# Head norms, rotary items and latent projections placed inside the mixers' input projection

## The reference

```python
    for l in range(DEPTH_2):
        x = x + 0.5 * swiglu(rms_norm(x, ffn1_norm[l]), ffn1_w_gate[l], ffn1_w_up[l], ffn1_w_down[l])
        h = rms_norm(x, mix_norm[l])
        pa, pb, pc, pd = jnp.split(h @ w_in[l], IN_SPLITS, axis=-1)
        ya = neighbourhood_mixer(pa, na_q_norm[l], na_k_norm[l], na_rpb[l], na_beta[l])
        yb = mla_mixer(pb, mla_q_lat_norm[l], mla_w_uq[l], mla_kv_lat_norm[l], mla_w_ukv[l],
                       mla_q_norm[l], mla_k_norm[l], mla_beta[l], ang_seq)
        yc = diff_mixer(pc, diff_q_norm[l], diff_k_norm[l], diff_lambda[l], diff_subln[l],
                        t5_bias, diff_lambda_init(l))
        yd = gqa_mixer(pd, gqa_q_norm[l], gqa_k_norm[l], gqa_beta[l], ang_row, ang_col)
        x = x + jnp.concatenate([ya, yb, yc, yd], axis=-1) @ w_out[l]
...
def mla_mixer(p, q_lat_norm, w_uq, kv_lat_norm, w_ukv, q_norm, k_norm, beta, ang):
    c_q, c_kv, k_rope = jnp.split(p, [MLA_Q_RANK, MLA_Q_RANK + MLA_KV_RANK], axis=-1)
    q = (rms_norm(c_q, q_lat_norm) @ w_uq).reshape(b, s, MLA_HEADS, MLA_NOPE + MLA_ROPE)
    kv = (rms_norm(c_kv, kv_lat_norm) @ w_ukv).reshape(b, s, MLA_HEADS, MLA_NOPE + MLA_V)
...
    q = rms_norm(q, q_norm)
    k = rms_norm(k, k_norm)
    q = jnp.concatenate([q[..., :MLA_NOPE], apply_rope(q[..., MLA_NOPE:], ang)], axis=-1)
    k = jnp.concatenate([k[..., :MLA_NOPE], apply_rope(k[..., MLA_NOPE:], ang)], axis=-1)
```

## Time and profile before

| what | value |
|---|---|
| median of 3 runs | 3502.92 us |
| lowest and highest run | 3497.03 and 3503.17 us |
| the profiled execution, its own time | 3499.19 us |
| span of the profiled execution | 3497.4 us |
| mean granted clock of TensorE | 0.957 of full |
| busy share: TensorE, VectorE, ScalarE, GpSimd | 95%, 50%, 37%, 6% |

### The profile page before, as it was taken

The page is one execution under the profiler, slowest core; times in us unless marked ns, Lnnn a source line. Parts: engine busy times, 40 slices in busy tenths (PEclk is TensorE's granted clock), DMA queues, the critical chain, the costliest instruction groups (busy, mean ns, idle before and its releaser), DMA issues.

```text
span 3497.4 us, 41394 instructions
## 1 busy us (share of the span) xinstructions
PE 3337.3 (95%) x15399; PEld 2655.9 (76%) x15399; DVE 1740.9 (50%) x2604; ACT 1299.6 (37%) x1853; POOL 213.4 (6%) x234
## 2 busy tenths in 40 slices
PE   8989987999999999999889999999999988999998
PEld 6667865888888888876478888878887646978887
DVE  7354467445553455333565555445553256555532
ACT  4226645224332333322247333333322233733322
POOL 1001100000000000010120100010001002010000
PEclk9959998999999999999789999999999987999999
DMA  5310012333333333332102333333333311223332
GB/s 125 96 42 4 1 55 67 97 91 96 96 94 94 101 96 94 89 106 67 47 20 65 95 97 95 89 94 96 96 95 93 91 53 17 67 73 97 98 94 67
DMA packets 518249, 275.12 MB, mean 79 GB/s; under 512 B 39523, under 2 KB 510407, under 8 KB 517986
## 3 DMA queue, kind: packets, MB, share of 16 engines
q1 hardware_dynamic: 513154, 262.77, 27.0%
q0 software_dynamic: 3600, 9.85, 0.9%
q10 hardware_dynamic: 1360, 0.66, 0.1%
HBM read 262.70 MB, written 2.14 MB: 76 GB/s over the span
## 4 chain that ended last, share of the span: by engine, by line
PE 89%; DVE 7%; ACT 2%; issue 1%; DMA 0%; POOL 0%; DVEq 0%; ACTq 0%; POOLq 0%
PE bank L375 24%; PE bank L377 24%; PE bank L376 24%; PE bank L1004 5%; PE bank L985 4%; PE bank L993 3%; PE bank L896 1%; PE bank L690 1%; PE bank L804 1%; DVE wlo L351 1%; PE bank L1679 1%; DVE xc L1886 0%; ACT whi L344 0%; DVE q L932 0%; DVE hhi L2183 0%
## 5 line engine op out<-in xcount | busy, mean ns | idle before, releaser
L375 PE MATMUL bank<-hhi,whi 128*128 128x512 f32 (+1 forms) x2528 | 1004.3, 397 | 38.0 <-DVEq L415 20.9
L376 PE MATMUL bank<-hhi,wlo 128*128 128x512 f32 (+1 forms) x2528 | 990.7, 392 | 0.0
L377 PE MATMUL bank<-hlo,whi 128*128 128x512 f32 (+1 forms) x2528 | 990.3, 392 | 0.0
L351 DVE TENSOR_TENSOR wlo<-raw,whi 128x1024 fp32r<-128x1024 f32 x485 | 607.2, 1254 | 621.9 <-ACT whi L344 613.3
L344 ACT CAST whi<-raw 128x1024 fp32r<-128x1024 f32 x485 | 505.0, 1046 | 428.4 <-PE bank L377 413.1
L375 PEld LDWEIGHTS bank<-hhi,whi 128*128 128x128 f32 (+1 forms) x2528 | 476.9, 189 | 184.2 <-issue 79.1
L376 PEld LDWEIGHTS bank<-hhi,wlo 128*128 128x128 f32 (+1 forms) x2528 | 477.3, 189 | 102.6 <-issue 3.5
L377 PEld LDWEIGHTS bank<-hlo,whi 128*128 128x128 f32 (+1 forms) x2528 | 476.8, 189 | 102.8
L375 PE MATMUL bank<-uhi,whi 128*128 128x512 f32 x880 | 348.9, 396 | 0.0
L376 PE MATMUL bank<-uhi,wlo 128*128 128x512 f32 x880 | 348.3, 396 | 0.0
L377 PE MATMUL bank<-ulo,whi 128*128 128x512 f32 x880 | 348.3, 396 | 0.0
(11 more groups left out here) (432 smaller groups left out, 3589.3 us busy)
## 6 DMA issues: line engine op xcount, KB each, us to landing
raw<-in_ffn_w_gate SPq DMA_DIRECT2D x88, 512.0 KB, 3.9
raw<-in_ffn_w_up SPq DMA_DIRECT2D x88, 512.0 KB, 3.7
raw<-in_w_in SPq DMA_DIRECT2D x78, 512.0 KB, 3.8
raw<-in_ffn_w_down SPq DMA_DIRECT2D x64, 512.0 KB, 3.9
raw<-in_w_out SPq DMA_DIRECT2D x24, 512.0 KB, 4.1
raw<-in_ffn_w_down SPq DMA_DIRECT2D x32, 384.0 KB, 3.4
raw<-in_w_gate SPq DMA_DIRECT2D x22, 512.0 KB, 3.9
raw<-in_w_up SPq DMA_DIRECT2D x22, 512.0 KB, 3.7
```

The source lines that it names most:

```text
L351: k.nc.vector.tensor_tensor(k.wlo[:, slot, :], k.raw[:, slot, :], k.whi[:, slot, :].bitcast(F32), ALU.subtract)\
L375: mm(out, whi, hi(kc), start=start and i == 0, stop=False)
L376: mm(out, wlo, hi(kc), start=False, stop=False)
L377: last = mm(out, whi, lo(kc), start=False, stop=stop and i == kcs - 1)
```

## The change

Parts 1 to 3 of `mix` become one stage without a handover inside, `mixer_inputs`. It has 22 units: three of B's latents, A's four queries and keys, B's rotary key (unit 7, `KR`), the two short latent units (8 and 9, `UQ`, `UKV`), D's, C's, and last the values (17 to 21). Each unit has two places for side work, called slots: slot 2u after half of unit u's matmuls, slot 2u+1 after the unit. Tables say what stands in which slot: `sums` (square sums), `spreads`, `rotations` (one slot behind the spread of a rotary item), `turns` (slots 20 to 23 for B's values, 36 to 39 for A's, 40, 42 and 44 for C's and D's), and the scales in four groups of heads (`roots`, `inverses`, `parts`). Every engine walks through the 45 slots in the same order. Spreads have one bank instead of two, transposes one instead of two. The latents' parts have buffers of their own, since `hhi` and `hlo` are in use. VectorE no longer copies the values' channels of the latents, ScalarE does. The cosine goes straight into the item's tile. The copies that gathered A's values on ScalarE are now four reads of the bank on VectorE for each of two units. The t5 table is loaded when the last unit is done, and GpSimd's bias additions wait for it. The exponential of lambda is in slot 41.

```diff
-        for c in range(4):
-            block(m2, 0, KC, O_A + c * P, P)
         for c in range(3):
             block(m2, 0, KC, O_B + c * P, P)
         for c in range(4):
-            block(m2, 0, KC, O_C + c * P, P)
+            block(m2, 0, KC, O_A + c * P, P)
+        block(m2, 0, KC, O_B + 384 - 64, 96)
+        block(rows_by_chunk(w["mla_w_uq_2"][l]), 0, 2, 0, 4 * MD)
+        block(rows_by_chunk(w["mla_w_ukv_2"][l]), 0, 1, 0, 4 * P)
...
+                    mixer_inputs(k, w, l, (qA, kA, vA), (qB, kB, vB), (qC, kC, vC), (qD, kD, vD), lat_parts, lam, gain,
+                                 lambda name, shape, dt=F32: sb(name, shape, dt, mem))
...
-            latent_heads(k, w, l, kr, qB, kB, vB, gain)
-            handover(k)
...
     def _(pool):
+        pool.wait_ge(*k.t5_landed.all())
         pool.wait_ge(*loaded)
...
+def mixer_inputs(k, w, l, near, latent, diff, shared, lat_parts, lam, gain, sb):
...
+    KR, UQ, UKV, VALUES, UNITS = 7, 8, 9, 17, 22
...
+    norm_of = {0: 11, 1: 12, 2: 13, 3: 0, 4: 1, 5: 2, 6: 3, 10: 8, 11: 9, 12: 10, 13: 4, 14: 5, 15: 6, 16: 7}
+    normed = [0, 1, 2, 3, 4, 5, 6] + [None] * 8 + [10, 11, 12, 13, 14, 15, 16]
+    sums = {2 * u + 3: [normed.index(u)] for u in norm_of}
+    sums.update({17 + i: [7 + 2 * i, 8 + 2 * i] for i in range(4)})
+    firsts, lasts = (0, 3, 7, 15), (2, 6, 14, 21)
+    group = lambda i: sum(i >= f for f in firsts) - 1
+    roots, inverses, parts = {7: 0, 15: 1, 21: 2, 35: 3}, {7: 0, 19: 1, 21: 2, 35: 3}, {8: 0, 20: 1, 22: 2, 36: 3}
...
+    spreads = {9 + i: i for i in range(3)}
+    spreads.update({21 + i: 3 + i for i in range(12)})
+    spreads.update({37 + i: 15 + i for i in range(7)})
+    rotations = {s + 1: i - 7 for s, i in spreads.items() if items[i]["rope"]}
...
+        def slot(s):
+            if s in rotations:
+                r = rotations[s]
+                rows = rope(r)["rows"]
+                pe.wait_ge(*k.xn_done.at(7 + r + 1))
+                if r >= 1:
+                    pe.wait_ge(*k.rope_sin.at(r))
+                if r == 8:
+                    pe.wait_ge(*gqa_ready)
+                nc.tensor.matmul(rotated[0:rows, :], rot[0:rows, 0:rows], tmp[0:rows, r % 2, :], start=True, stop=True)\
+                    .then_inc(*k.rot_done.up())
+            if s in spreads:
+                i = spreads[s]
+                it, g = items[i], group(i)
+                if i == 0:
+                    pe.wait_ge(*tables_ready)
+                if i in firsts:
+                    pe.wait_ge(*k.rn_ready.at(2 * g + 2))
+                if i:
+                    pe.wait_ge(*k.xn_done.at(i))
+                table, heads = (backm, 8) if g == 2 else (back, NORM2_HEADS)
+                for part in scales[g % 2]:
+                    last = nc.tensor.matmul(spread_bank[0:it["rows"], :], table[0:heads, it["norm"], 0:it["rows"]],
+                                            part[0:heads, :], start=part is scales[g % 2][0],
+                                            stop=part is scales[g % 2][1])
+                last.then_inc(*k.spread_done.up())
...
+        def beside(u):
+            def before(i):
+                if u == 0:
+                    inputs(i)
+                if i == KC // 2:
+                    slot(2 * u)
+            return before
...
+            else:
+                pe.wait_ge(k.acc_read.sem, c0 + chunk(u) - 3)
+                cols = MD if u == KR else P
+                products(k, bank(chunk(u))[0:cols, :], at, KC, cols, 0, lambda j: k.hhi[:, j, :],
+                         lambda j: k.hlo[:, j, :], before=beside(u)).then_inc(k.units_done.sem, 1)
+            if u == 0 and k.sum_squares:
+                k.sum_squares(pe)
+            slot(2 * u + 1)
+        slot(2 * UNITS)
...
+            if s in spreads:
+                i = spreads[s]
+                it = items[i]
+                rows, out = it["rows"], it["tile"]
+                if it["rope"]:
+                    r = i - 7
+                    out = tmp[0:rows, r % 2, :]
+                    if r < 2:
+                        dve.wait_ge(k.tiles_turned.sem, t0 + r + 3)
+                    else:
+                        dve.wait_ge(*k.rope_out.at(r - 1))
...
+            if s in rotations:
+                r = rotations[s]
+                rows, out = rope(r)["rows"], rope(r)["tile"]
+                if r >= 1:
+                    dve.wait_ge(*k.rope_out.at(r))
+                if r == 8:
+                    dve.wait_ge(*gqa_ready)
+                dve.wait_ge(*k.rot_done.at(r + 1))
+                nc.vector.tensor_tensor(tmp[0:rows, 2, :], rotated[0:rows, :], sin[0:rows, :], ALU.mult)\
+                    .then_inc(*k.rope_sin.up())
+                dve.wait_ge(*k.rope_sin.at(r + 1))
+                dve.wait_ge(*k.rope_cos.at(r + 1))
+                nc.vector.tensor_tensor(out, out, tmp[0:rows, 2, :], ALU.add).then_inc(*k.rope_out.up())
...
+            pool.wait_ge(*k.xn_done.at(7 + r + 1))
+            nc.gpsimd.tensor_tensor(out, tmp[0:rows, r % 2, :], cos[0:rows, :], ALU.mult).then_inc(*k.rope_cos.up())
...
+        pool.wait_ge(k.units_done.sem, n0 + UNITS)
+        pool.wait_ge(k.tables_out, 32)
+        pool.dma_start(t5, bass.AP(k.t5_dram.tensor, 0, [[1, P], [1024, 4], [1, 896]]).bitcast(F32R))\
+            .then_inc(*k.t5_landed.up(by=16))
```

More of the change, by code:

```diff
@@ L285, in plan_weights @@
         block(m2, 0, KC, O_D + 256, P)
+        for c in range(4):
+            block(m2, 0, KC, O_C + c * P, P)
         for c in (4, 5):
             block(m2, 0, KC, O_A + c * P, P)
-        block(m2, 0, KC, O_B + 384 - 64, 96)
         for c in (4, 5):
@@ L1991, in sb @@
             return mem.enter_context(nc.sbuf_tensor(k.name(name), shape, dt, side=side))
-        with ExitStack() as qk, ExitStack() as kr_mem:
+        with ExitStack() as qk:
             qsb = lambda name, shape: sb(name, shape, F32, qk)
+            with ExitStack() as lat_mem:
+                lat_parts = [sb(n, [P, 3, T], F32R, lat_mem) for n in ("lat_hi", "lat_lo")]
+            vA, vC, vB, vD = (qsb(n, [P, tiles, heads, HD + 1]) for n, tiles, heads in
+                              (("vA", 8, 4), ("vC", TB, 4), ("vB", TB, 4), ("vD", TB, 2)))
@@ L1995, in mix @@
             qA, kA, qC, kC = (qsb(n, [P, 2, T]) for n in ("qA", "kA", "qC", "kC"))
[L1996 to L1998 removed]
+            qD, kD = qsb("qD", [P, 2, T]), qsb("kD", [P, T])
             lam, gain = qsb("lam", [P, P + 8]), qsb("gain", [P, 4])
[L2000 to L2012, removed]
[L2013 to L2084 removed]
@@ L2089, in mix @@
-            handover(k)
-            kr_mem.close()
             ytok = sb("ytok", [P, TB, D], side="right")
@@ L2319, in lambda_init @@
     return 0.8 - 0.6 * math.exp(-0.3 * l)
-def diff_lambda(k, lam, l):
-    nc = k.nc
-    s = lambda i, n=1: lam[:, P + i:P + i + n]
-    @k.block.vector
-    def _(dve):
-        for i in range(2):
-            a, b = lam[:, 64 * i:64 * i + 32], lam[:, 64 * i + 32:64 * i + 64]
-            nc.vector.tensor_tensor_reduce(out=a, in0=a, in1=b, scale=1.0, scalar=0.0, op0=ALU.mult, op1=ALU.add,
-                                           accum_out=s(i)).then_inc(*k.lam_dot.up())
-    dots = k.lam_dot.all()
-    @k.block.scalar
-    def _(act):
-        act.wait_ge(*dots)
-        nc.scalar.activation(s(2, 2), s(0, 2), ACT.Exp).then_inc(*k.lam_exp.up())
-    done = k.lam_exp.all()
-    @k.block.vector
-    def _(dve):
-        dve.wait_ge(*done)
-        nc.vector.tensor_tensor(s(4), s(3), s(2), ALU.subtract).then_inc(*k.lam_dot.up())
-        dve.wait_ge(*k.lam_dot.all())
-        nc.vector.tensor_scalar(s(5), s(4), -lambda_init(l), None, ALU.add)
 def bias_views(k, ytok):
@@ L2653, in build @@
         k.into_landed = signal("into_landed")
-        k.x_odd = signal("x_odd")
+        k.x_odd, k.vt_copied, k.t5_landed = signal("x_odd"), signal("vt_copied"), signal("t5_landed")
         k.start_landed, k.ones_landed = signal("start_landed"), signal("ones_landed")
```

412 lines of the change are left out of this document (261 added, 151 removed).

## The result

| what | value |
|---|---|
| before, median of 4 runs beside it | 3503.05 us |
| after, median of 4 runs | 3457.73 us (3454.41 to 3462.87) |
| ratio, 95% interval | 0.9883 [0.9862, 0.9904] |
| span before, after | 3497.4, 3456.9 us |
| forecast | 3433 us, range 3418 to 3462 |

It is faster, as forecast, but by 1.2% where 2% was forecast. The median lies inside the range and 25 us above the predicted time; by the ratio (0.9883 x 3503.05 = 3462) the change stands at the range's upper end. The spans differ by 40.5 us where the sum had 69.4.

A forecast was written before the change was run, and what follows sets the result against it. TensorE was taken as the bound, with 89% of the span. Per layer 76.3 - 39.0 - 1.0 - 3.1 + 1.5 = 34.7 us, both layers 69.4, from 3499.2 to 3429.8, plus 3.7 for the median: 3433 us, range 3418 to 3462.

The forecast's parts named there:

- What goes: Stretch from the input projection's end to the attention's first cast, expected to disappear: 76.3 us per layer.
- the added work: Latent units, sums, spreads, rotations, transposes and stream breaks that TensorE gets inside the projection: 39.0 us per layer.
- A rotary unit: Steady unit of the new stage with two rotations, two spreads and a sum: 10.0 us of TensorE with breaks.
- Waits in the stage: TensorE waiting for side work inside the new stage: 1.0 us per layer, ends 0.6 and 10.
- The tail: From the last unit's end to the attention's first cast: 3.1 us per layer, with the t5 load hidden.
- Behind the stage: GpSimd's bias additions, now waiting for the t5 table, may slip by 4 us at zero cost.
- The clock: Attention's first 15 matmuls run at half clock for a shorter while: 1.5 us gained per layer, ends 0 and 3.2.
- Hand-overs: Rival: filled slots in the stage make TensorE wait 0.3 us each, 19 us in both layers: 3452; chance 0.22.
- the lock in the stage: Rival: GpSimd's eleven cosines per layer lock out VectorE in the stage, 28 us in all: 3461; chance 0.08.
- the two signs: For the lock: VectorE's low parts and sums well over 1.22 and 0.69 us, with TensorE waiting behind them.

The follow-up runs named there:

- both: Changed kernel with the t5 table loaded by SyncE behind the wide loads and GpSimd's bias additions held until VectorE's last split of B: 3415.00 us.
- pause_4: `both` plus TensorE made to wait, ahead of scores in the attention, until GpSimd has done three zeroings: 3453.95 us.
- bias_before: Kernel before the change, with only GpSimd's bias additions held until VectorE has split B's four heads: 3485.23 us.
- late_bias: Changed kernel with GpSimd's bias additions held until VectorE has split B's four heads, first zeroing in their middle: 3427.13 us.
- one_place: Changed kernel with slot 2u's side work ahead of unit u's first matmul instead of in its middle (UQ apart): 3459.60 us.

## Why the prediction was right and wrong

The prediction had the new stage right to a microsecond and two things behind it wrong: what GpSimd's load does to the tail, and what the clock does in the attention.

- **What goes, 76.3 us, and the added work, 39.0: right.** The stage was to take 122.25 + 39.0 + 1.0 = 162.25 us from the third unit's start to the last unit's end and took 161.90. A rotary unit, forecast at 10.0, took 9.85. The sums and rotations cost 0.97 and 0.95 us each:

```profile
1647.07 1.02 PE L2349 MATMUL bank<-ntmp,rot 96*96 96x512 f32 x2
1648.02 0.47 PE L2362 MATMUL bank<-rhi,backm 8*96 8x512 f32 x1
...
1656.92 1.02 PE L2349 MATMUL bank<-ntmp,rot 96*96 96x512 f32 x2
1657.87 0.47 PE L2362 MATMUL bank<-rhi,backm 8*96 8x512 f32 x1
```

- **Waits in the stage, 1.0 us with 0.6 at the first scales: right.** The wait there was 0.51 and the only one up to the last unit's end; the next, 0.28 us, is in the tail.
- **The tail, 3.1 us: wrong, it was 7.96.** The step that failed is "GpSimd's load of the t5 table (one issue) is given out at the last unit's end and hides behind it". I priced the issue and not what stands behind it on GpSimd, its drain at the handover. The trace before held the hint: that load stood in the middle of a part there, 44 us ahead of the next first cast. The term was mis-sized by 2 x 4.9 = 9.7 us. With the load elsewhere the whole piece from the third unit's start to the first cast, forecast at 165.4, took 1722.55 - 1558.21 = 164.3 (`both`).
- **Behind the stage, additions "may slip by 4 us for nothing: zero": right as a difference, wrong as a reading.** They slipped by 1.1 us against the first scores (9.25 us behind them instead of 8.19). Beside them the two casts of B's last head took 0.97 and 0.94 us, in the kernel before 0.55 and 0.95; the subtractions took 1.10 and 1.20 in after, and before 1.11 and the 1.20 of the earlier trace rows. The wait of step 9 was there in both kernels. I compared the additions' end with their first reader and left out whom they slow down: held back, they save 17.4 us before the change and 33.4 after it.
- **The clock, +1.5 us per layer, ends 0 and 3.2: wrong by its sign.** The step that failed is that the clock behind the stage could only give something back ("ends 0 and 3.2"). I looked at the first 15 matmuls only. They did gain, 6.38 to 5.44 us in layer 0, but not in layer 1 (6.66 before, 6.77 after). The bounds left out that the clock may fall once more while the heads run: a wait that had cost its own length before was now followed by half clock, for 27 and 31 us. Measured: 6.0 and 10.7 us lost. This is the larger miss, 19.7 of the 28.9 us between 69.4 and 40.5; the tail is 9.7, and the stage's other terms gave 0.5 back.
- **Rivals.** Hand-overs (3452) and the lock in the stage (3461) lie nearest to the measured time, for the wrong reason: neither made TensorE wait in the stage. The lock itself did take place there. VectorE's sum of a rotary item took 1.28 us where the next item's cosine ran beside it on GpSimd, in nine of the eleven items of layer 0 (the two of 128 partitions 1.29 and 1.30), and 0.69 where none did:

```profile
1649.65 1.29 POOL L2590 TENSOR_TENSOR qB<-ntmp,cos 96x512 f32<-96x512 f32 x1 [4.07 <-DVE ntmp L2547]
1650.21 1.28 DVE L2561 TENSOR_TENSOR qB<-qB,ntmp 96x512 f32<-96x512 f32 x1
...
1682.92 0.69 DVE L2561 TENSOR_TENSOR kB<-kB,ntmp 96x512 f32<-96x512 f32 x1
```

  That is some 0.6 us each, 5 us of VectorE's time in a layer, and VectorE's slack took it: of the two signs that the prediction gives for this rival, longer sums came and TensorE behind them did not. The Trainium skill (SBUF — State Buffer, section SBUF: two separate sides) has the lock as exclusive for a whole instruction, and for a VectorE instruction with two SBUF inputs only against a GpSimd instruction that reads SBUF. The rows agree with both: the casts of 2.96 and 2.10 us above, the sums beside a cosine, and in `both` a subtraction with two SBUF inputs, which took its usual 0.68 us beside a zeroing, which only writes.

```profile
1745.69 2.08 POOL L2062 MEMSET hhi<- 64x2048 f32 x1 [1.91 <-PE bank L985]
...
1746.06 0.68 DVE L2113 TENSOR_TENSOR hhi<-qA,hhi 64x512 fp32r<-64x512 f32 x1
```

## What to carry to other kernels

When a stage is shortened, read the first 60 us behind it as closely as the stage: which side work of GpSimd now lies beside which of VectorE's steps, and what TensorE's short waits there do to its clock. Here a transfer that GpSimd issued just ahead of a handover was waited for in full; issued by ScalarE at the same point it cost nothing there. And before a wait of two microseconds is called small, ask what clock follows it: here, where the clock fell, such a wait cost six to twelve times its length, and where it didn't, about its length.

## What the runs showed of the hardware

- GpSimd's drain at the end of a block lasted until its own transfer of 1792 KB had landed (7.38 and 7.64 us); with the load issued by ScalarE at the same point, or by SyncE behind the handover, and typed `F32`, the wait ahead of the first cast was 0.81 to 0.86 us.
- TensorE stayed at half clock for 27 us and more while its rows show it busy without a gap (46.00 of 46 in `pause_4`, layer 1), with the small matmuls of attention. Being busy did not bring the clock back at once.
- A cast of VectorE, 0.42 us alone, took 2.96 and 2.10 us beside GpSimd's zeroings and up to 0.97 us beside its additions of 0.85 us each. A sum with two SBUF inputs took 1.28 us beside a GpSimd multiplication of 1.29 us, and 0.69 alone.
- Kernels without the wait repeat within 2 to 5.5 us (`bias_before`, `both`, `late_bias`), those with it within 3 to 23. The longest runs have the lowest mean granted clock: 0.963 in the 3478.97 of `one_place` against 0.967 to 0.970 in its others, 0.962 in the 3464.80 of `pause_4` against 0.966. So the clock was lost in some executions and not in others; where in the program is known only for the profiled ones.
